# Scores of the first block's attention as three passes over high and low parts made on GpSimd, with x reloaded after the last score

## What is computed

```python
q_r = apply_rope(q, cos, sin)
k_slc = apply_rope(k_slc, cos, sin)
k_win = apply_rope(k_win, cos, sin)
...
s = jnp.einsum('bqghd,bgqkd->bghqk', qr, ks) * scale      # selected keys
p = masked_softmax(s, (kpos <= t[:, None])[:, :, None])
o_slc = jnp.einsum('bghqk,bgqkd->bqghd', p.astype(vs.dtype), vs)
...
s = jnp.einsum('bqghd,bkgd->bghqk', qr, kw) * scale       # window keys
p = masked_softmax(s, wmask)
o_win = jnp.einsum('bghqk,bkgd->bqghd', p.astype(vw.dtype), vw)
return g[..., 0:1] * o_cmp + g[..., 1:2] * o_slc + g[..., 2:3] * o_win
...
mix = jnp.concatenate([attn, ssm], axis=-1) @ w_out
return x + gate[:, None, :] * mix
```

## Time and profile before

| what | value |
|---|---|
| median of 3 runs | 906.72 us (906.34 to 906.87) |
| profiled execution, its own time | 905.98 us |
| profiled execution, its span on the core | 904.2 us |
| TensorE busy | 875.7 us, 97% of the span |
| VectorE busy | 578.9 us, 64% |
| ScalarE busy | 450.7 us, 50% |
| GpSimd busy | 99.7 us, 11% |
| granted TensorE clock, mean | 0.997 of full speed |

### The profile page before, as it was taken

One profiled execution on the slowest core, in us unless ns is written; L12 is line 12 of the kernel. 1 busy time (PEld: TensorE's weight loads), 2 busy tenths in 40 slices (PEclk: granted clock), 3 DMA queues, 4 the chain that ended last, 5 costly groups with the idle time before them and its releaser, 6 DMA issues.

```text
span 904.2 us, 14652 instructions
## 1 busy us (share of the span) xinstructions
PE 875.7 (97%) x5733; PEld 708.0 (78%) x5733; DVE 578.9 (64%) x1154; ACT 450.7 (50%) x956; POOL 99.7 (11%) x121
## 2 busy tenths in 40 slices
PE   3999999999999999999999999999999999999996
PEld 1579888784677778788888888888888888888885
DVE  5899797989888564666465455345476556445533
ACT  4734323386787334465535466234366554555531
POOL 1001112012400000000010232000000001131202
PEclk9999999999999999999999999999999999999998
DMA  9836655347200313323223424122322332342203
GB/s 384 335 98 140 176 159 168 125 133 240 94 2 2 116 62 118 118 88 95 71 94 116 141 94 131 51 94 94 120 88 67 94 106 96 125 140 71 84 10 94
DMA packets 34678, 104.69 MB, mean 116 GB/s; under 512 B 14961, under 2 KB 14961, under 8 KB 32178
## 3 DMA queue, kind: packets, MB, share of 16 engines
q1 hardware_dynamic: 28098, 85.77, 28.5%
q0 software_dynamic: 3856, 15.73, 5.5%
q10 hardware_dynamic: 2656, 2.26, 1.0%
HBM read 98.37 MB, written 4.19 MB: 113 GB/s over the span
## 4 chain that ended last, share of the span: by engine, by line
PE 92%; DVE 4%; ACT 2%; DMA 1%; issue 1%; SPq 0%; POOL 0%; POOLq 0%; ACTq 0%; DVEq 0%
PE bank L1101 85%; PE bank L1461 2%; PE bank L1615 2%; PE bank L1441 2%; DMA ring<-in_w_ada 1%; PE bank L1501 1%; DVE arena L1749 1%; PE bank L1491 0%; ACT arena L768 0%; DVE xn_t L2271 0%; DVE ring_lo L2295 0%; DVE w_lo L2243 0%; ACT soft L861 0%; DVE pw L1743 0%; DVE x_t L2331 0%
## 5 line engine op out<-in xcount | busy, mean ns | idle before, releaser
L2243 DVE TENSOR_TENSOR w_lo<-ring,w_hi 128x1024 fp32r<-128x1024 f32 x80 | 101.4, 1270 | 51.8 <-ACT w_hi L943 49.3
L1101 PE MATMUL bank<-hT_hi,w_hi 128*128 128x512 f32 x320 | 129.4, 404 | 0.0
L1101 PE MATMUL bank<-hT_lo,w_hi 128*128 128x512 f32 x320 | 125.2, 391 | 0.0
L1101 PE MATMUL bank<-hT_hi,w_lo 128*128 128x512 f32 x320 | 124.9, 390 | 0.0
L1101 PE MATMUL bank<-w_hi,hT_hi 128*128 128x512 f32 x256 | 101.7, 397 | 0.3 <-DVE hT_lo L2289 0.3
L1101 PE MATMUL bank<-w_lo,hT_hi 128*128 128x512 f32 x256 | 99.9, 390 | 0.0
L1101 PE MATMUL bank<-w_hi,hT_lo 128*128 128x512 f32 x256 | 99.8, 390 | 0.0
L943 ACT ACTIVATE w_hi<-ring 128x1024 fp32r<-128x1024 f32 x80 | 84.3, 1057 | 14.0 <-PE bank L1101 13.8
L1101 PEld LDWEIGHTS bank<-hT_hi,w_hi 128*128 128x128 f32 x320 | 60.1, 188 | 16.8 <-issue 4.7
L1101 PEld LDWEIGHTS bank<-hT_lo,w_hi 128*128 128x128 f32 x320 | 60.1, 188 | 13.1
L1101 PEld LDWEIGHTS bank<-hT_hi,w_lo 128*128 128x128 f32 x320 | 60.2, 188 | 11.2
(11 more groups left out here) (341 smaller groups left out, 1834.3 us busy)
## 6 DMA issues: line engine op xcount, KB each, us to landing
ring<-in_w_units SPq DMA_DIRECT2D x80, 512.0 KB, 3.7
ring<-in_w_ada SPq DMA_DIRECT2D x4, 2048.0 KB, 10.3
bias_ring<-in_na_bias POOLq DMA_DIRECT2D x6, 1024.0 KB, 5.2
ring<-in_w_out SPq DMA_DIRECT2D x2, 2048.0 KB, 8.8
bias_ring<-in_t_bias POOLq DMA_DIRECT2D x8, 448.0 KB, 3.7
x_t<-in_x SPq DMA_DIRECT2D x4, 512.0 KB, 5.7
arena<-in_w_ada SPq DMA_DIRECT2D x1, 2048.0 KB, 19.9
arena<-in_w_ada SPq DMA_DIRECT2D x2, 1024.0 KB, 22.8
```

The source lines that it names most:

```text
L1101: return pe.matmul(out, lhsT, rhs, start=first, stop=last)
L2243: dve.tensor_tensor(w_lo[:, u % 4], raw_w[:, u % 4], w_hi[:, u % 4].bitcast(fp32), SUB).then_inc(S["w_split"], 1)
```

## The change

`score_1` now runs three fp32r passes for each pair (high queries by high keys, low queries by high keys, high queries by low keys), in the form that `na_score` has in the second block. GpSimd makes the parts: a cast to the high part and a subtraction for the low part, for 4 token blocks of queries and 4 tiles of keys (2 branches by 2 groups), each of 512 numbers a partition. The order is: queries of block 3, the four key tiles, queries of blocks 2, 1 and 0. The high parts lie in `x_hi`, the low parts over the raw queries and keys. A semaphore `qk_split` counts one step of ScalarE (the last move of `move_q(3)`) and then the eight splits; the first pair waits for 4 of them, the first pair of the window branch for 6, blocks 2, 1 and 0 for 7, 8 and 9. As `x_hi` holds the high parts until the last score, the reload of x moves in GpSimd's list from ahead of the stage to behind its split of w_out, with a wait until VectorE has taken the last of the 64 heads.

```diff
@@ -123,7 +123,10 @@
-            sbm("arena_gap", SG * (LC + 1) * SC + 2 * GP * NCH + 2048 + 2304)
+            sbm("arena_gap", SG * (LC + 1) * SC)
+            kT_lo = cut(sbm("kT_lo", 2 * GP * NCH)[:, :], a=2 * NG, t=T)
+            sbm("tmp_gap", 2048)
+            qTr_lo = cut(sbm("qTr_lo", 2304)[:, 0:2048], h=4, t=T)
@@ -196,9 +199,8 @@
-        ksT = cut(rot_c, g=NG, t=T)
-        kwT = cut(rot_s, g=NG, t=T)
         kT_all = cut(rot_cs, a=2 * NG, t=T)
+        qTr_hi, kT_hi = x_hi[:, 0:4], x_hi[:, 4:KD]
@@ -563,9 +565,21 @@
             pool.wait_ge(S["proj_done"], PT_ZA + 4)
-            for i in range(NT):
-                pool.dma_start(x[:, i, :], io["x"].rearrange("(r c) f -> c r f", r=GROWS)[16 * i:16 * (i + 1)]).then_inc(S["x_back"], 16)
-
+            pool.wait_ge(S["qk_split"], 1)
+
+            def split_qk(hi, lo, raw):
+
+                settle(pool.tensor_copy(hi, raw))
+                pool.tensor_tensor(lo, raw, hi.bitcast(fp32), SUB).then_inc(S["qk_split"], 1)
+
+            def split_q(i):
+                split_qk(*(v[:, :, i * P:(i + 1) * P] for v in (qTr_hi, qTr_lo, qTr)))
+
+            split_q(NT - 1)
+            for a in range(2 * NG):
+                split_qk(kT_hi[:, a, :], kT_lo[:, a, :], kT_all[:, a, :])
+            for i in reversed(range(NT - 1)):
+                split_q(i)
             pool.wait_ge(S["ssm_ready"], 4)
@@ -577,6 +591,9 @@
                 ins.then_inc(S["wo_lo"], 1)
+            pool.wait_ge(S["s1_taken"], 2 * len(PAIRS1))
+            for i in range(NT):
+                pool.dma_start(x[:, i, :], io["x"].rearrange("(r c) f -> c r f", r=GROWS)[16 * i:16 * (i + 1)]).then_inc(S["x_back"], 16)
@@ -811,8 +828,7 @@
-                if i < NT - 1:
-                    ins.then_inc(S["q_evac"], 1)
+                ins.then_inc(S["q_evac" if i < NT - 1 else "qk_split"], 1)
@@ -1362,13 +1378,16 @@
             def score_1(j):
                 i, br, heads_ = PAIRS1[j]
-                kT = kwT if br else ksT
                 if j >= 2:
                     pe.wait_ge(S["s1_taken"], 2 * j - 2)
-                for k, h in zip((2 * j, 2 * j + 1), heads_):
-                    hf = slice((h % 2) * HD, (h % 2 + 1) * HD)
-                    mm(bank[S_BANKS[k % 4]][:, 0:(i + 1) * P], qTr[hf, h // 2, i * P:(i + 1) * P], kT[hf, h // 4, 0:(i + 1) * P], True, True)\
-                        .then_inc(S["s1_done"], 1)
+                pe.wait_ge(S["qk_split"], (6 if br else 4) if i == NT - 1 else 9 - i)
+                for n, (q_, k_) in enumerate(((qTr_hi, kT_hi), (qTr_lo, kT_hi), (qTr_hi, kT_lo))):
+                    for k, h in zip((2 * j, 2 * j + 1), heads_):
+                        hf = slice((h % 2) * HD, (h % 2 + 1) * HD)
+                        ins = mm(bank[S_BANKS[k % 4]][:, 0:(i + 1) * P], q_[hf, h // 2, i * P:(i + 1) * P],
+                                 k_[hf, 2 * br + h // 4, 0:(i + 1) * P], n == 0, n == 2)
+                        if n == 2:
+                            ins.then_inc(S["s1_done"], 1)
```

More of the change, by code:

```diff
@@ L270, in build @@
             "cs_exp", "cp_ready", "cp_T", "cp_evac", "gate_tanh",
-            "s1_done", "s1_taken", "e1_done", "p1_scaled", "t1_done", "t1_evac", "o1_done", "mix_out", "ssm_lo", "mix_hi", "mix_lo", "wo_hi", "wo_lo", "wo_used", "scores_done", "scores_taken",
+            "qk_split", "s1_done", "s1_taken", "e1_done", "p1_scaled", "t1_done", "t1_evac", "o1_done", "mix_out", "ssm_lo", "mix_hi", "mix_lo", "wo_hi", "wo_lo", "wo_used", "scores_done", "scores_taken",
             "exp_done", "mixed", "pT_done", "pT_evac", "o_done", "o_used", "mixT_done", "mixed_hi",
```

## The result

The changed kernel takes 909.15 us (median of 8 runs, 908.62 to 910.28), the kernel before on the same chip 906.41 (8 runs, 905.43 to 906.87): 1.0033 times as long, 95% interval 1.0023 to 1.0042, so 2.7 us slower. Its profiled execution has a span of 907.4.

The account below looks back on a forecast made before the run. VectorE was taken to bound the stage until 227 us, TensorE behind it. Splits +4.5, passes -2.1 and 128-column pairs +1.3 gave +3.7, so 909.7 on the profiled execution and 910.4 for the median, range 904.0 to 913.8.

Parts of the forecast that it names:

- VectorE is the bound ahead of 227: Stage up to 227 us: VectorE is full, so TensorE savings there (1.3) count as nothing; those behind count.
- the granted clock should stay at 1.00: Sign of being right: TensorE's clock stays at 1.00; a fall in the new gaps would add to the loss.
- Splits, +4.5: From 197.5 to about 220, GpSimd's eight splits hold VectorE's two-input instructions, 4.5 late at 227; bounds 2.3 to 8.7.
- the walk: Going down GpSimd's and VectorE's instruction lists from 197.5, each waiting for the other: delays of 5.1, less 0.6 idle absorbed.
- only subtractions hold: Lower bound of the split term: GpSimd's casts do not hold VectorE, about 2.2 go, leaving 2.3.
- Three passes behind 227, -2.1: TensorE's pairs behind 227, one of 512 columns, eight each of 384 and 256: 0.18 + 1.1 + 0.8 = 2.1 saved.
- 128-column pairs, +1.3: Eight 128-column pairs: between saving 1.0 (half a 256-column pass) and losing 3.5 (plain rate), middle taken: +1.3.
- The reload, 0: Late reload of x: issued by 286.6, lands 3.8 later at 290.4, before the first residual sum at 296.43; no cost.
- TensorE stays the bound: Rival: VectorE is not late, passes save behind and partly ahead of 227: -2.7, 904.0; chance 0.15 (faster).
- the two cancel: Rival: only subtractions hold (2.3) and narrow passes are cheap: 906.7, no change; chance 0.20.
- narrow passes at the plain rate: Rival: 128-column passes lose 3.5 on top of VectorE's delay: +5.9, 912.6; chance 0.11.
- x is late: Rival: the reload lands at 300.0, after the first residual sum could start: +6.3, 913.0; chance 0.04.

Follow-up runs that it names:

- the memsets: Changed kernel with plain float32 scores, each GpSimd cast and subtraction replaced by a memset of about its length: 906.76 against 906.4 before, 1.0007.
- the splits alone: Changed kernel with its eight splits and late reload of x kept, but plain float32 scores and the parts unused: 911.18 against 905.94 before, 1.0052.
- the reload alone: Kernel before with only the reload of x moved behind the last score: 906.38 against 905.94, 1.0001.
- three query tiles later: Changed kernel with five splits made ahead, the third query tile's behind ssm_out, two behind the old splits: 910.75 against 906.4 before, 1.0053.
- casts on ScalarE: Changed kernel with the eight casts made by ScalarE, GpSimd only subtracting: 911.36 against 906.4 before, 1.0059.
- the last kernel: Changed kernel with three query tiles split later and ScalarE's fourth tanh moved ahead of its first exponentials: 907.98 against 906.0 before, 1.002.

## Why the prediction was right

The forecast was 910.4, and 909.15 was measured; the side was right, and so was the mechanism: what GpSimd reads holds VectorE, and that costs more than the passes save. The place at which TensorE comes to wait was wrong, and two sizes were met in part by luck. Point by point:

- **VectorE is the bound ahead of 227.** Right: the chain that ended last in the changed kernel runs almost wholly through VectorE and ScalarE from 199 to 230. But it was half of it. The prediction had TensorE idle at 2.0 or more in `turn_1(2)` and `turn_1(3)`; it waited 0.94 there, as before, and 0.46. Its wait comes earlier. The fourth tanh stands on ScalarE behind exponentials that wait for the first take, which is 2.6 late. So TensorE stood 2.36 and then ran for some 3 us at the lower clock, against "the granted clock should stay at 1.00"; with the 1.7 that the 16 matmuls lost there, this alone makes TensorE about 4.0 late. At the third pair the two chains are level: TensorE's score starts at 219.56, before at 214.90, 4.1 late; VectorE's take at 220.56, before at 216.06, 4.0 late. That fits the two experiments: taking away VectorE's holds behind 210 left the loss (910.75), and taking away the gap as well brought 907.98. The gap alone was not taken away.
- **Splits, +4.5.** 4.8 of holds against the 5.1 of the walk, and 4.0 of delay at `turn_1(3)`. That the sums are so close is in part luck. The walk had three instructions that were not held at all: the small product behind line 2157 (0.7 in the walk), `scale_1(0)` (0.95) and `ssm_out(2)` (1.45), the last two because GpSimd was done at 217 and not at 220. It left out the two small `TENSOR_SCALAR`s (0.72 and 0.55) and had too little for line 2164 (0.35, measured 1.09) and for `ssm_out(0)` and `ssm_out(1)` (0.95, measured 2.1). And the 4.0 are reached by two routes, of which it saw one. The bound "only subtractions hold" (2.3) is excluded by the row at 202.32, and the memsets show that it is reading which holds the two-input instructions. The first score waited to 205.18, for 205.1 forecast. Beside plain scores the splits cost 5.2: there the granted clock was 0.66 at 210 to 220, and 0.83 with the passes, and VectorE stood 1.39 for TensorE at the third take, where it did not wait in the changed kernel. Why the clock stayed low for longer there no run shows.

```profile
221.35 0.69 DVE L2241 CUSTOM_DVE_ANT_0 soft<-bank,cq 128x512 f32<-128x512 f32 x1 [1.39 <-PE bank L1124]
```

- **Three passes behind 227, -2.1.** Two pairs of 384 columns take 1.25 (1.49 in the trace of before), two of 256 take 0.91 (1.07), one of 512 about 0.8, as in the earlier trace rows. The sum, 0.2 + 8 x 0.12 + 8 x 0.08, is 1.8: the term was 0.3 too large.
- **128-column pairs, +1.3.** They take 0.40 (0.32), 0.65 lost by the eight. The term was twice what was measured: a pass costs 0.11 at 128 columns and 0.12 at 256, so it follows neither the width nor the plain rate.
- **The reload, 0.** Right in the time, and nearly wrong in its reason. The forecast took 3.8 to land from the other 512 KB transfers on this queue; the four of x, issued within 2.4 of one another, took 5.0 to 9.2, with a median of 7.1. So x was there only at 298.9, 8.7 behind the last issue, where the prediction has x decide from 9.8 on. VectorE's wait of 1.25 ahead of the first residual sum ended with x in the changed kernel, where a wait of the same length ended with TensorE before: "VectorE waiting for x after its last split of w_out", one of the signs of being wrong, did come, at no cost. The first residual sum is as late as the rest, 2.7 with the 0.54 off.

```profile
298.94 0.69 DVE L1762 TENSOR_TENSOR soft<-bank,gate_b 128x512 f32<-128x512 f32 x1 [1.25 <-DMA x_t<-in_x]
```

- **The sum.** 4.0 - 1.8 + 0.65 = +2.85, where +2.7 was measured and +3.7 forecast: all three terms were too large, the two losses by 0.5 and 0.65 and the saving by 0.3, so that part of the errors cancelled.
- **The rivals.** "TensorE stays the bound" and "the two cancel" fell with the splits alone at +5.2; "narrow passes at the plain rate" with 0.40 a pair; "x is late" with the time of the reload alone, though x did come after TensorE there.

## What to carry to other kernels

Work for an idle GpSimd is not free where VectorE is full: count which VectorE instructions with two SBUF inputs will run beside what GpSimd reads, and add up their surplus (4.8 here, 1.3 of it on two one-input `TENSOR_SCALAR`s, which were held as well). Whether a hold costs anything depends on which engine is later at that point (4.3 of holds at 220 to 236 cost 0.4 at most, 6.3 at 241 to 257 cost 1.8), and an engine's idle time in a stretch doesn't tell. When an engine is made late, follow each of its consumers: two of them may become late by the same amount, as VectorE and TensorE did here (4.0 and 4.1), and then mending one alone shows nothing.

## What was not expected of the hardware

- The passes of a group cost from start to start 0.23 at 512 columns, 0.17 at 384, 0.12 at 256, and still 0.11 at 128.
- A `TENSOR_SCALAR` of 32 columns, 0.18 alone, took 0.90 beside a subtraction and 0.83 beside a memset that reads nothing, while 128x1024 two-input instructions ran their 1.23 beside memsets. The Trainium skill ("SBUF — State Buffer", section "Who interferes with whom") tells the two cases apart: two SBUF inputs against GpSimd's reads, and a two-port mode, which it says a `tensor_scalar` can enter, against any use of the shared ports. The memsets agree with both; that this instruction ran in such a mode no row shows.
- After a gap of 2.36 in which TensorE ran nothing, with the clock still 1.00 in it, the granted clock fell to 0.50 (1.2 GHz) for some 3 us while it worked, and 16 matmuls took 3.61 for 1.92. With the gap closed they took 1.92 at 1.00. Behind the gaps of 2.43 (splits alone), 2.35 (three query tiles later) and 4.07 (casts on ScalarE) the clock fell to 0.50 too; behind one of 0.94 in the last kernel it did not.
